# Up and gate projections of three MLPs by pairs of chunks, with seven half-width block products for eight

## What is computed

```python
def swiglu(u, w_gate_up, w_down):          # D_FF = 2816
    gate, up = jnp.split(u @ w_gate_up, 2, axis=-1)
    return (jax.nn.silu(gate) * up) @ w_down

def sqrelu_mlp(x, w1, w2):                 # D_FF_2 = 4096, twice
    h = jax.nn.relu(x @ w1)
    return (h * h) @ w2
```

## Time and profile before

| | us |
|---|---|
| median of 3 runs | 2213.63 |
| lowest, highest | 2213.21, 2213.8 |
| span of the profiled execution | 2211.5 |
| TensorE busy in it | 2179.2 |
| VectorE, ScalarE, GpSimd busy | 1262.7, 855.4, 359.4 |

### The profile page before, as it was taken

How to read it: one execution, slowest core, us unless ns; L and a number is a source line. 1 busy time by engine, 2 the same in 40 slices (tenths; PEclk the granted TensorE clock), 3 DMA queues, 4 the chain that set the end, 5 groups by cost and what they waited for, 6 DMA issues and landing times.

```text
span 2211.5 us, 27926 instructions
## 1 busy us (share of the span) xinstructions
PE 2179.2 (99%) x10904; PEld 1730.0 (78%) x10904; DVE 1262.7 (57%) x1953; ACT 855.4 (39%) x1414; POOL 359.4 (16%) x364
## 2 busy tenths in 40 slices
PE   8999999999999999999999999999989999999998
PEld 6888788878888888766688888888865568888886
DVE  5866565654444445487655555566567755555553
ACT  4433464443222224465542222234426753222223
POOL 2301330010000004165310000010136631000001
PEclk9999999999999999999999999999999999999999
DMA  5233125223333332211033333333410013333331
GB/s 173 84 103 95 39 86 172 67 68 95 97 98 98 96 97 86 86 48 48 29 102 98 95 96 95 96 95 118 121 49 1 1 39 95 96 96 96 96 95 48
DMA packets 292659, 187.78 MB, mean 85 GB/s; under 512 B 7856, under 2 KB 286768, under 8 KB 292528
## 3 DMA queue, kind: packets, MB, share of 16 engines
q1 hardware_dynamic: 292240, 185.78, 28.2%
q10 hardware_dynamic: 288, 0.21, 0.0%
HBM read 183.88 MB, written 2.10 MB: 84 GB/s over the span
## 4 chain that ended last, share of the span: by engine, by line
PE 94%; DVE 2%; ACT 2%; issue 1%; DMA 0%; POOL 0%; ACTq 0%; DVEq 0%
PE ps L470 92%; PE ps L504 2%; ACT wh L456 0%; DVE wl L466 0%; DVE tmp L1101 0%; ACT XH L491 0%; ACT p_xscr L654 0%; DMA p_xt<-in_x 0%; DVE sb_small L2937 0%; DVE st_Ll L2297 0%; ACT xb_x L491 0%; DVE H L614 0%; ACT st_L L2249 0%; DVE xb_x L2592 0%; DVE st_L L2281 0%
## 5 line engine op out<-in xcount | busy, mean ns | idle before, releaser
L466 DVE TENSOR_TENSOR wl<-raw,wh 128x1024 fp32r<-128x1024 f32 x336 | 421.6, 1255 | 589.1 <-ACT wh L456 588.7
L456 ACT CAST wh<-raw 128x1024 fp32r<-128x1024 f32 x336 | 349.2, 1040 | 633.0 <-PE ps L470 620.6
L470 PE MATMUL ps<-XH,wh 128*128 128x512 f32 x1072 | 424.9, 396 | 4.7 <-issue 3.6
L470 PE MATMUL ps<-XH,wl 128*128 128x512 f32 x1072 | 418.9, 391 | 0.0
L470 PE MATMUL ps<-XL,wh 128*128 128x512 f32 x1072 | 418.0, 390 | 0.0
L470 PE MATMUL ps<-xb_x,wh 128*128 128x512 f32 x1088 | 339.3, 393 | 0.4 <-DVE H L614 0.3
L557 POOL TENSOR_TENSOR acc<-acc,sq 128x512 f32<-128x512 f32 x55 | 78.6, 1429 | 1320.4 <-ACT sq L547 1319.4
L470 PEld LDWEIGHTS ps<-XH,wh 128*128 128x128 f32 x1072 | 201.2, 188 | 48.3 <-issue 4.7
L470 PEld LDWEIGHTS ps<-xb_x,wh 128*128 128x128 f32 x1088 | 203.1, 188 | 45.0 <-issue 1.1
L470 PEld LDWEIGHTS ps<-XH,wl 128*128 128x128 f32 x1072 | 200.9, 187 | 44.0
L470 PEld LDWEIGHTS ps<-XL,wh 128*128 128x128 f32 x1072 | 201.3, 188 | 41.5 <-issue 0.7
(11 more groups left out here) (397 smaller groups left out, 3452.9 us busy)
## 6 DMA issues: line engine op xcount, KB each, us to landing
raw<-in_mlp_w SPq DMA_DIRECT2D x128, 512.0 KB, 3.7
raw<-in_w_gate_up SPq DMA_DIRECT2D x44, 512.0 KB, 3.7
raw<-in_w_in SPq DMA_DIRECT2D x29, 512.0 KB, 3.7
raw<-in_sb_w_qkv SPq DMA_DIRECT2D x24, 512.0 KB, 3.6
raw<-in_w_down SPq DMA_DIRECT2D x22, 512.0 KB, 3.4
raw<-in_w_out_mix SPq DMA_DIRECT2D x16, 512.0 KB, 3.4
raw<-in_w_kv SPq DMA_DIRECT2D x16, 512.0 KB, 3.7
raw<-in_nsa_w_kv SPq DMA_DIRECT2D x12, 512.0 KB, 3.5
```

The costliest lines, as they stand in the source:

```text
L456: e.copy(shaped(WH[i % NH], i), shaped(RAW[i % NR], i)).then_inc(*w_hi.up(i))
L466: e.tensor_tensor(shaped(WL[i % NH], i), shaped(RAW[i % NR], i), shaped(WH[i % NH], i).bitcast(F), ALU.subtract).then_inc(*w_lo.up(i))
L470: return e.matmul(out, a, b, start=start, stop=stop, skip_group_check=True)
```

## The change

A pair of neighbouring chunks is one job (`gates` or `ups`). The weights of the pair are seen as 2 x 2 blocks (two chunks, even and odd k tiles), the activations as 2 x 2 blocks (even and odd k tiles, the first 256 tokens and the last 256). The four block results are then made of seven block products, p1 to p7, for eight: some of them multiply sums of blocks. A block product is 4 k tiles x 3 matmuls of 256 columns. 51 pairs are made so: 10 of gates and 11 of ups in `ff`, 15 of ups in each of `fm` and `fn`. The first two chunks of each MLP stay single.

- **Weights.** A pair has two loads (a and b) and four operands: `:22` (half of b, 128x512), `:1` (all of a), and `:12` and `:43`, sums of blocks that GpSimd makes of the loads in four additions and subtractions of 128x512 (`pool_sums`). Each operand is split by ScalarE and VectorE as before. A load's buffer is free once its split and the second sum are made. NH goes from 3 to 4.
- **Activations.** In the projection before an MLP, ScalarE copies each new tile of `H` with the gain of the norm (`act_turned_in`), GpSimd makes four combinations of 128x256 for every second tile (`pool_combine`), and ScalarE and VectorE split these (128x1024, `act_combined`, `dve_combined`), the last of them inside the MLP, at its job 1. GpSimd also makes the sums of the first pair there, between its sums of squares.
- **Eviction.** ScalarE copies p1 with p4 (128x512), p5 and p6 (128x256) from PSUM to `Q4`. Products p3, p6 and p7 go on in the bank that these lay in: p6 waits for the copy of p1, p3 for that of p5, p7 for that of p6. VectorE forms the two chunks, one after p3 (`sum_a`), one after p7 (`sum_b`), scales each by the norm, multiplies or squares, and splits. `self.steps` sets at which later job each of these is done: within one or two jobs for gates and where more pairs follow, spread over the next four jobs where downs follow.
- **Order.** All pairs of a group stand on end, then come the eight downs of the group ahead, as before; in `act` and `dve` weights are now made up to three operands ahead. The buffers of several stages change place (the attention that follows the gated MLP reads `XB`), and the copy of the hidden tiles has buffers of its own.

```diff
-    NR, NH = 5, 3
+    NR, NH = 5, 4
...
+    def unit_pair(name, ap0, ap1):
+        b, a = raw(name + "b", ap1), raw(name + "a", ap0)
+        before = pairs_of.get("last")
+        q0 = operand(name + ":22", "odd", b, [4, 128])
+        q1 = operand(name + ":1", "unit", a, [8, 128])
+        operand(name + ":12", "sum", (name, 0), [8, 128])
+        operand(name + ":43", "sum", (name, 1), [8, 128])
+        raw_done[b] = [(w_lo, (q0,)), (g_made, ("wsum", name, 1))]
+        raw_done[a] = [(w_lo, (q1,)), (g_made, ("wsum", name, 1))]
+        pairs_of[name] = (a, b, q0, before)
+        pairs_of["last"] = name
...
+    def ffn_jobs(gated, groups):
+        def pair(g, c):
+            return [("gates", g, c), ("ups", g, c)] if gated else [("ups", g, c)]
+        def downs(g, o0, o1):
+            return [("down", g, o) for o in range(o0, o1)]
+        last = len(groups) - 1
+        if gated:
+            jobs = [("gate", 0, 0), ("gate", 0, 1), ("ups", 0, 0)]
+        else:
+            jobs = [("up", 0, 0), ("up", 0, 1), ("ups", 0, 2)]
+        for g in range(1, last + 1):
+            c = sum(groups[:g])
+            jobs += pair(g, c) + pair(g, c + 2) + downs(g - 1, 0, 8)
+        return jobs + downs(last, 0, 8)
...
+    def pool_sums(e, name):
+        a, b, q0, before = pairs_of[name]
+        ta, tb = raw_tile(a), raw_tile(b)
+        e.wait_ge(*w_in[b % NR].at(b))
+        if before:
+            e.wait_ge(*w_lo.at(UI[before + ":12"]))
+        e.tensor_tensor(SU[0][:, 0:4, :], tb[:, 0::2, :], tb[:, 1::2, :], ALU.add).then_inc(*g_made.up())
+        e.wait_ge(*g_made.now())
+        e.wait_ge(*w_in[a % NR].at(a))
+        e.tensor_tensor(SU[0][:, 4:8, :], SU[0][:, 0:4, :], ta[:, 0::2, :], ALU.subtract).then_inc(
+            *g_made.up("wsum", name, 0))
+        if before:
+            e.wait_ge(*w_lo.at(UI[before + ":43"]))
+        e.tensor_tensor(SU[1][:, 4:8, :], ta[:, 0::2, :], tb[:, 0::2, :], ALU.subtract).then_inc(*g_made.up())
+        e.wait_ge(*g_made.at("wsum", name, 0))
+        e.tensor_tensor(SU[1][:, 0:4, :], ta[:, 1::2, :], SU[0][:, 4:8, :], ALU.subtract).then_inc(
+            *g_made.up("wsum", name, 1))
...
+                act_turned_in(e, "ff", o - 1, col("ffn_norm", o - 1))
+                if o >= 3 and o % 2:
+                    act_combined(e, "ff", (o - 3) // 2)
...
+            if o % 2:
+                pool_combine(e, "ff", o // 2)
+            if o == 5:
+                ff.pool_first(e)
...
+    def act_turned_in(e, tag, k, gain):
+        j = k // 2
+        if k % 2 == 0 and j:
+            e.wait_ge(*g_made.at("tf", tag, j - 1))
+        e.activation(tb2[k % 2][:, :], H[:, k, :], ACT.Copy, scale=gain).then_inc(*a_made.up("tb", tag, k))
+    def pool_combine(e, tag, j):
+        e.wait_ge(*a_made.at("tb", tag, 2 * j))
+        e.wait_ge(*a_made.at("tb", tag, 2 * j + 1))
+        if j:
+            e.wait_ge(*x_lo.at("t" + tag, j - 1))
+        b1, b2 = ([t[:, 0:256], t[:, 256:512]] for t in tb2)
+        e.tensor_tensor(tf[:, 0, :], b1[1], b1[0], ALU.subtract).then_inc(*g_made.up())
+        e.wait_ge(*g_made.now())
+        e.tensor_tensor(tf[:, 1, :], b2[1], tf[:, 0, :], ALU.subtract).then_inc(*g_made.up())
+        n = g_made.now()
+        e.tensor_tensor(tf[:, 2, :], b2[1], b1[1], ALU.subtract).then_inc(*g_made.up())
+        e.wait_ge(*n)
+        e.tensor_tensor(tf[:, 3, :], b2[0], tf[:, 1, :], ALU.subtract).then_inc(*g_made.up("tf", tag, j))
+    def act_combined(e, tag, j):
+        e.wait_ge(*g_made.at("tf", tag, j))
+        e.copy(TT.hi[:, j, :, :], tf[:, :, :]).then_inc(*x_hi.up("t" + tag, j))
+    def dve_combined(e, tag, j):
+        e.wait_ge(*x_hi.at("t" + tag, j))
+        e.tensor_tensor(TT.lo[:, j, :, :], tf[:, :, :], TT.hi[:, j, :, :].bitcast(F), ALU.subtract).then_inc(
+            *x_lo.up("t" + tag, j))
...
+                    quick = kind == "gates" or self.jobs[n + 1][0] != "down" and self.jobs[n + 2][0] != "down" or g == 0
+                    for step, lag in zip(("sum_b", "scale_a", "scale_b", "act_a", "act_b", "low_a", "low_b"),
+                                         (1, 1, 1, 1, 1, 2, 2) if quick else (1, 1, 2, 2, 3, 3, 4)):
+                        self.steps[n + lag].append((step, n))
...
+        def product(self, e, n, part, q, w, out, x, first):
+            e.wait_ge(*w_lo.at(q))
+            wh, wl = shaped(WH[q % NH], q), shaped(WL[q % NH], q)
+            for j in range(4):
+                xh, xl = x(j)
+                k = w + j if U[q][0] != "unit" else w + 2 * j
+                mm(e, out, wh[:, k, :], xh, first and j == 0, False)
+                mm(e, out, wh[:, k, :], xl, False, False)
+                f = mm(e, out, wl[:, k, :], xh, False, j == 3)
+            f.then_inc(*proj.up(self.tag, part, n))
...
+            self.product(e, n, "p4", q, 0, A_[:, 256:512], combined(3), True)
+            done(0)
+            self.product(e, n, "p1", q + 1, 0, A_[:, 0:256], block(0, 0), True)
+            self.product(e, n, "p2", q + 1, 1, C_[:, 0:256], block(1, 0), True)
+            done(1)
+            self.product(e, n, "p5", q + 2, 0, C_[:, 256:512], combined(0), True)
+            e.wait_ge(*a_made.at(tag, "p1", n))
+            self.product(e, n, "p6", q + 2, 4, A_[:, 0:256], combined(1), False)
+            done(2)
+            e.wait_ge(*a_made.at(tag, "p5", n))
+            self.product(e, n, "p3", q + 3, 0, C_[:, 256:512], block(1, 256), False)
+            e.wait_ge(*a_made.at(tag, "p6", n))
+            self.product(e, n, "p7", q + 3, 4, A_[:, 0:256], combined(2), False)
+            done(3)
...
+        def act_pair(self, e, n):
+            tag, q = self.tag, self.first(n)
+            A_, C_ = got((tag, "A", n)), got((tag, "C", n))
+            before = [b for b in range(n) if self.paired(b)]
+            act_weights(e, q + 4)
+            e.wait_ge(*proj.at(tag, "p1", n))
+            if before:
+                e.wait_ge(*v_made.at(tag, "sum_a", before[-1]))
+                e.wait_ge(*v_made.at(tag, "sum_b", before[-1]))
+            e.copy(Q4[:, 0:2, :], A_[:, :]).then_inc(*a_made.up(tag, "p1", n))
+            e.wait_ge(*proj.at(tag, "p5", n))
+            e.copy(Q4[:, 3, :], C_[:, 256:512]).then_inc(*a_made.up(tag, "p5", n))
+            e.wait_ge(*proj.at(tag, "p6", n))
+            e.copy(Q4[:, 2, :], A_[:, 0:256]).then_inc(*a_made.up(tag, "p6", n))
+            act_weights(e, q + 6)
...
+        def dve_sum_a(self, e, n):
+            tag = self.tag
+            t = take(e, self.tile(n, 0))
+            e.wait_ge(*proj.at(tag, "p3", n))
+            e.wait_ge(*a_made.at(tag, "p6", n))
+            e.tensor_tensor(t[:, :].rearrange("p (a t) -> p a t", a=2), Q4[:, 0::2, :],
+                            got((tag, "C", n))[:, :].rearrange("p (a t) -> p a t", a=2), ALU.add).then_inc(
+                *v_made.up(tag, "sum_a", n))
+        def dve_step(self, e, step, n):
+            tag, m = self.tag, int(step[-1] == "b")
+            kind, g, c = self.jobs[n]
+            if step == "sum_b":
+                t = take(e, self.tile(n, 1))
+                e.wait_ge(*proj.at(tag, n))
+                e.wait_ge(*a_made.at(tag, "p5", n))
+                u3 = got((tag, "A", n))[:, 0:256].unsqueeze(1).to_broadcast([128, 2, 256])
+                e.tensor_tensor(t[:, :].rearrange("p (a t) -> p a t", a=2), Q4[:, 1::2, :], u3, ALU.add).then_inc(
+                    *v_made.up(tag, "sum_b", n))
+                return
+            t = got(self.tile(n, m))
+            if step[:5] == "scale":
+                e.wait_ge(*a_made.at("rs", self.norm))
+                e.wait_ge(*v_made.at(tag, "sum_" + step[-1], n))
+                e.tensor_tensor(t[:, :], t[:, :], rs[:, :], ALU.mult).then_inc(*v_made.up(tag, step, n))
...
+            elif kind == "ups" and step[:3] == "act":
+                e.wait_ge(*v_made.at(tag, "scale_" + step[-1], n))
+                self.dve_hidden(e, c + m)
+            elif kind == "ups":
+                dve_lo(e, self.hid[g % 2], f"{tag}{g}", c + m - self.c0(g), t[:, :])
...
+                for step, b in self.steps[n]:
+                    self.dve_step(e, step, b)
+                if self.paired(n):
+                    dve_weights(e, self.first(n) + 6)
+                    self.dve_sum_a(e, n)
```

342 lines of the change are left out of this document (220 added, 122 removed).

## The result

| | before | after |
|---|---|---|
| median, us (4 runs each) | 2213.42 | 2228.56 |
| lowest to highest | 2212.99 to 2213.80 | 2227.71 to 2228.88 |
| span of the profiled execution | 2211.5 | 2227.0 |

The ratio is 1.0068 (95% interval 1.0056 to 1.008): the kernel became slower by 0.7%, where 1.8% faster was forecast and 2206 was the upper end of the range.

A forecast was written before the change was run, and what follows sets the result against it. The prediction took TensorE's matmuls to bound the kernel, busy 2179 of 2211.5 us. It summed 2211.5 - 59 + 15 + 4 = 2171.5 of span, with 2.1 around it 2174 us, 1.8% less; range 2155 to 2206.

The forecast's parts named there:

- TensorE's own part: In the pairs: 84 half-width matmuls replace 48, 1.16 us less a pair, -59 us over 51 pairs.
- D: Rival on TensorE in pairs: half-width matmuls stand less dense, 0.127 us each, 2217 us in all; chance 0.11.
- E: Rival on TensorE in pairs: each load of weights must end before the next, 2459 us; chance 0.02.
- VectorE and GpSimd: In pairs the two take turns: no loss in `fm` and `fn`, 3 us per gated group, +15 us (0 to 20).
- Rival C: In the gated MLP VectorE sets the pace, each gated pair 3.3 us over TensorE's time: 2228 us; chance 0.09.
- Starts of the MLPs: In projections ahead of MLPs, added GpSimd and VectorE work delays TensorE's first job: 1.3 us each, +4 us (0 to 12).
- At nothing: Terms priced at zero: ScalarE's 6.3 of 9.8 us a pair, the loads, the fourth weight buffer, the attention's moved buffers.

The follow-up runs named there:

- nosums: Kernel after, but GpSimd makes sums of weights only for each MLP's first pair, and all other pairs split these again: 2202.86 us.
- startonly: Kernel after with every chunk single and no pairs; the combinations of activations are still made in the projections ahead, never used: 2234.28 us.
- sumb: Kernel after, but VectorE does `sum_b` ahead of the low parts of the pair before: 2217.63 us.
- nocomb: Kernel after, but combinations of activations are made only for the first two tiles of `H`, and all pairs read these: 2199.18 us.
- late2s: Kernel after with groups 0 and 1 single, combinations made inside the MLP, pairs from group 2 on, `sum_b` ahead of low parts: 2173.99 us.
- filler: Kernel after, with TensorE multiplying 33 extra, overwritten matmuls while it waits in the first job of `ff` and `fm`: 2231.21 us.

## Why the prediction was wrong, point by point

**TensorE's own part** was right in kind, a seventh too large. Product starts in after, in the second MLP, 12 steps apart (two lines with x2 stand for two matmuls):

```profile
1242.93 0.28 PE L537 MATMUL ps<-tt_t,wl 128*128 128x256 f32 x1
...
1244.34 0.28 PE L537 MATMUL ps<-xb_x,wl 128*128 128x256 f32 x1
```

1.41 / 12 = 0.1175, the 0.117 of the earlier trace rows; a whole pair goes at 0.118. Two pairs take 19.8 us against 21.8 for four single chunks: 1.0 a pair and not 1.16 (the 0.229 of the earlier trace rows was 0.227 over a whole group), so -51 us for 51 pairs and not -59. Rivals D and E are out. The Trainium skill's figures for the distance ("TensorE: Matmul & The Clock Gate", section "Back-to-back issue gap") do not fit after either: 0.118 us at 256 columns is close to what it has for 512.

**VectorE and GpSimd** were right, and their price too high: they take turns in pairs (splits of 2.00 and 1.96 beside GpSimd, 1.22 without), `fm` and `fn` lose nothing, a group of `ff` in full swing loses 1.0 us (40.96 for its four pairs, against 43.95 - 4.0) to 1.4 (by nosums), where I had taken 3. The gaps stand ahead of p6 behind the copy of p1, as named. Rival C is not what made it slower, though its 2228 is what was measured: it asked for 3 us at every gated pair, and past the starts a whole group has two gaps of 0.4 and 0.5: the equal number is chance. The Trainium skill ("SBUF — State Buffer", section "SBUF: two separate sides") says that the pair of ports that the two engines share is held whole, by an operation of VectorE with two inputs from SBUF too. The trace agrees (GpSimd's sum at 506.17 took 2.25 us, the two ahead of it 1.27 and 1.26), and it holds for the combinations as well, which I had priced without turns.

**Starts of the MLPs** is the step that failed: +4 (0 to 12) was foreseen, and +3 for the one gated group in that stretch, about 62 measured. Three things in it were wrong.
- The time per two tiles. I took two projections of a later stage, 11.0 us. In the trace of before, ScalarE's rows for every second tile ahead of the first MLP stand 8.66 us apart, and GpSimd's 10.8 us don't fit in that even without turns. Ahead of the second MLP it is the same, and only ahead of the third do two projections take 11.0 (1831.67 to 1842.65). That fits startonly, where the combinations cost 10.6, 10.2 and 1.6 us; but the third start lost 13 in after all the same (10.2, and its three pairs), so this point is not the whole. The rows:

```profile
487.99 0.72 ACT L491 ACTIVATE xb_x<-H,cols 128x512 fp32r<-128x512 f32 x1 [2.14 <-DVE H L614]
...
496.65 0.72 ACT L491 ACTIVATE xb_x<-H,cols 128x512 fp32r<-128x512 f32 x1 [2.15 <-DVE H L614]
```

In after, the first pair's sums with the sums of squares and combinations beside them kept GpSimd busy for 17.9 us on end.

- The queues. I summed busy time per engine, and asked of none what stands behind the new instruction. L1895 waits for GpSimd, and ahead of the weights; L1918 waits for L1914, and ahead of the next tile's addition to `H`. A late combination thus delays tile 7's addition, the low parts of tiles 6 and 7, and the norm, though nobody needs the combination yet. Behind these stands the fence, at which both engines wait for all of GpSimd's work in the projection (6.46 us for 2.11 on ScalarE). I had this question for the pairs, where it led me right, and not for the start.
- The first group. I priced gaps in the pairs alike everywhere, and nothing at all in `fm` and `fn`. The first group of `ff` had 3.5 and 3.2 us where later ones have 0.5: low parts that stand ahead of `sum_b` meet GpSimd's sums there. Without the sums (nosums), or with `sum_b` first (sumb), these two gaps are gone; without the combinations (nocomb) they stay. The first pair of `fm` has another, of 2.9 us at 1185.15: ScalarE's copy of p1 (1184.53) stands behind the cast of the last single chunk (1183.48), for which ScalarE had waited 3.20 us.

How much each of these is worth alone can't be said to the microsecond: 29 us went with the combinations, 26 with the sums, 11 with one step's place, 7 with the first pair's, and they overlap.

**At nothing.** The loads hid, as foreseen: no wait of TensorE goes to one. ScalarE's copy of p1 was late behind `sum_b` and at first pairs, which is priced above. That the clock would fall was not foreseen at all.

## What to carry to other kernels

A stage start has the least slack in the kernel: work that only prepares a later stage belongs where the engines have a whole group of time ahead of its reader, even if a fifth of the gain goes with it (late2s, 40 pairs for 51, won 1.8% where after lost 0.7%). Price such a move by queue: for each engine write down what stands behind the new waiting instruction and who needs that. And take the length of a stretch from the rows of that stretch, not of one that looks alike.

## What the runs showed of the hardware

- **The clock after a wait.** In before it never fell inside an MLP. In after it was 0.50 for 13.65 us from 504.8 on (TensorE had waited 2.0 us at 501 and was 0.7 into a wait of 5.0), and it stayed low to 518.4; from 509.0 on TensorE had waited once, 0.88 us ahead of 513.24. Its matmuls of 512 columns stood 0.43 us apart in it (515.96 to 516.39), for 0.227. The Trainium skill ("TensorE: Matmul & The Clock Gate", section "What's actually happening") says that the gate is low by default and activity releases it; the trace agrees, filler above all: with 33 more matmuls in the wait the clock was 1.00 there.
- **What it costs depends on who sets the time.** With the clock up in that stretch filler was 2.7 us slower than after and not faster, for the norm's factor came at 523.35 as at 523.53. Where TensorE set the pace, behind the factor, the same matmuls took 26.6 us with 9 of them at 0.50, and 25.2 with 3.4 at 0.50.
- **Turns hold small operations too**: a combination of 0.73 us took 1.59 beside a split (GpSimd, 500.22), so GpSimd's short operations are held by VectorE's long ones, and not only the other way round.
